# Fewer ordinary gate/up pairs in the SwiGLU stages of a four-layer streaming encoder, and the token-half sums moved within them

## The reference, cut to what matters

```python
def swiglu_ffn(x, w_in, w_out):
    g, u = jnp.split(x @ w_in, 2, axis=-1)
    return (jax.nn.silu(g) * u) @ w_out

    xp = xp + swiglu_ffn(rmsnorm(xp, ffn_norms[i]), *ffn_params[i])
...
y_prompt = rmsnorm(xp, final_norm)
```

## Time and profile before

| | us |
|---|---|
| median of 3 runs | 2585.49 |
| lowest, highest | 2583.73, 2587.84 |
| the profiled execution, device time | 2584.34 |
| its span in the profile | 2582.6 |
| PE busy | 2549.6 (99%) |
| PEld busy | 2483.3 (96%) |
| DVE busy | 1688.8 (65%) |
| ACT busy | 1179.4 (46%) |

### The profile page before, as it was taken

The page is one execution under the profiler, slowest core; times in us unless marked ns, Lnnn a source line. Parts: engine busy times, 40 slices in busy tenths (PEclk is TensorE's granted clock), DMA queues, the critical chain, the costliest instruction groups (busy, mean ns, idle before and its releaser), DMA issues.

```text
span 2582.6 us, 48134 instructions
## 1 busy us (share of the span) xinstructions
PE 2549.6 (99%) x20065; PEld 2483.3 (96%) x20065; DVE 1688.8 (65%) x2465; ACT 1179.4 (46%) x1778; POOL 171.9 (7%) x182
## 2 busy tenths in 40 slices
PE   8999999999999999999999999999999999999998
PEld 8999999999988899999998899999999999999998
DVE  5555793884555579479557556947955555884872
ACT  5454551543555555245345644524524553541443
POOL 2101000001000010000112210000011101000001
PEclk9999999999999999999999999999999999999999
DMA  4222333332433233333222222333322223333322
GB/s 117 70 76 82 99 93 96 99 95 73 124 99 104 77 92 96 91 102 93 84 69 80 72 86 76 97 98 93 100 81 79 72 73 90 98 92 96 94 84 80
DMA packets 441634, 230.68 MB, mean 89 GB/s; under 512 B 16884, under 2 KB 437968, under 8 KB 441440
## 3 DMA queue, kind: packets, MB, share of 16 engines
q1 hardware_dynamic: 439792, 226.89, 30.7%
q10 hardware_dynamic: 1200, 0.59, 0.1%
q0 software_dynamic: 448, 0.45, 0.1%
HBM read 219.03 MB, written 8.87 MB: 88 GB/s over the span
## 4 chain that ended last, share of the span: by engine, by line
PE 95%; DVE 3%; issue 1%; ACT 1%; DMA 0%; DVEq 0%; ACTq 0%
PE slot L2255 53%; PE aux L2734 14%; PE slot L2734 14%; PE aux L2255 4%; PE aux L2223 2%; PE aux L2636 1%; PE aux L2400 1%; PE aux L2642 1%; PE aux L2548 1%; PE aux L2486 1%; DVE w_lo L1397 1%; PE aux L2415 1%; PE aux L2418 0%; PE slot L2695 0%; PE aux L2290 0%
## 5 line engine op out<-in xcount | busy, mean ns | idle before, releaser
L734 ACT ACTIVATE w_hi<-raw 128x1024 fp32r<-128x1024 f32 (+5 forms) x231 | 265.3, 1148 | 346.9 <-PE slot L2255 315.0
L2255 PE MATMUL slot<-xg_hi,w_hi 128*128 128x272 f32 x1856 | 401.8, 298 | 12.5 <-DVE w_lo L1397 10.0
L2255 PE MATMUL slot<-xg_hi,w_lo 128*128 128x272 f32 x1856 | 383.8, 288 | 0.0
L2255 PE MATMUL slot<-xg_lo,w_hi 128*128 128x272 f32 x1856 | 383.7, 288 | 0.0
L1397 DVE TENSOR_TENSOR w_lo<-raw,w_hi 128x1024 fp32r<-128x1024 f32 (+4 forms) x229 | 309.7, 1352 | 69.3 <-ACT w_hi L734 68.6
L2255 PEld LDWEIGHTS slot<-xg_hi,w_hi 128*128 128x128 f32 x1856 | 291.1, 189 | 25.1 <-DVE w_lo L1397 12.4
L2255 PEld LDWEIGHTS slot<-xg_lo,w_hi 128*128 128x128 f32 x1856 | 291.9, 189 | 0.0
L2255 PEld LDWEIGHTS slot<-xg_hi,w_lo 128*128 128x128 f32 x1856 | 290.8, 189 | 0.0
L2255 PE MATMUL slot<-h_hi,w_hi 128*128 128x272 f32 x1386 | 286.1, 288 | 0.7 <-issue 0.7
L2255 PE MATMUL slot<-h_hi,w_lo 128*128 128x272 f32 x1386 | 285.9, 287 | 0.0
L2255 PE MATMUL slot<-h_lo,w_hi 128*128 128x272 f32 x1386 | 285.6, 287 | 0.0
(11 more groups left out here) (391 smaller groups left out, 5859.3 us busy)
## 6 DMA issues: line engine op xcount, KB each, us to landing
raw<-in_l_ffn_w_out_dram SPq DMA_DIRECT2D x64, 704.0 KB, 4.6
raw<-in_l_ffn_w_in_dram SPq DMA_DIRECT2D x72, 512.0 KB, 4.6
raw<-in_l_gla_w_in_dram SPq DMA_DIRECT2D x48, 512.0 KB, 3.8
ffn_raw_b<-in_l_ffn_w_in_dram SPq DMA_DIRECT2D x70, 256.0 KB, 3.5
ffn_raw_b<-in_l_ffn_w_in_dram SPq DMA_DIRECT2D x35, 512.0 KB, 5.2
raw<-in_l_ffn_w_in_dram SPq DMA_DIRECT2D x68, 256.0 KB, 3.3
raw<-in_l_att_w_qkv_dram SPq DMA_DIRECT2D x24, 512.0 KB, 3.8
raw<-in_l_lru_w_in_dram SPq DMA_DIRECT2D x24, 512.0 KB, 3.8
```

Source lines behind the costliest of these rows:

```text
L734: act.activation(w_hi[par][:, 0:kt, :], raw[par][:, 0:kt, :], ACT.Copy).then_inc(s_hi, 1)
L2255: ins = pe.matmul((slot[par] if bank is None else bank)[:, hf, 0:HALF], w[par][:, k, :], a[:, k0 + k, hf * HALF:(hf + 1) * HALF], start=(k ...
```

## The change

Half 0 has now two ordinary pairs and nine seven-product pairs (before 3 and 8), half 1 eleven seven-product pairs (before 1 and 10), and half 1 of the last layer eleven as well (before 4 ordinary and 7 seven-product). Quarters 0 and 1 of t stand in window 0 ahead of the read and the split, quarter 2 in window 0 behind them, quarter 3 in window 1. In half 1 the first pair's weight sums are formed in the last window of down0. The last half's h is no longer multiplied by rstd; its down stage does it, in a read and an add per block.

```diff
-UP_PAIRS = ("CCCSSSSSSSS", "CSSSSSSSSSS")
-LAST_PAIRS = "CSSCSSCSSCS"
-T_PART = {0: (0,), 1: (1, 2), 2: (3,)}
+UP_PAIRS = ("CCSSSSSSSSS", "SSSSSSSSSSS")
+LAST_PAIRS = "SSSSSSSSSSS"
+T_PART = {0: ((0, 1), (2,)), 1: ((3,), ())}
...
         def next_k(i, name):
+            if name == "down0" and up_kinds(i, 1, layers)[0] == "S":
+                return "seven"
...
 # ACT, last_project
-                    act.wait_ge(s_free, b0 + m + 1)
+                    act.wait_ge(s_xd, XT * (2 * i + 1) + m + 1)
...
 # ACT, project_out
-                        split(b0 + m2 * 2 + (j + 1), (p0 + j + 1) % 2, nxt if j else kt)
+                        if j and nxt == "seven":
+                            hi_sums((i, 1, 0), b0 + XT, None)
+                            hi_more_sums((i, 1, 0), b0 + XT, None)
+                        else:
+                            split(b0 + m2 * 2 + (j + 1), (p0 + j + 1) % 2, nxt if j else kt)
...
 # ACT, up_window (DVE's the same with t_low)
-                for q in T_PART.get(u, ()) if hf == 0 else ():
+                for q in T_PART[u][0] if hf == 0 and u in T_PART else ():
                     t_high(i, q)
...
                     split(b + 2, p0, XT if nxt else FH)
                 if now == "C":
                     silu(i, hf, u, kinds)
+                for q in T_PART[u][1] if hf == 0 and u in T_PART else ():
+                    t_high(i, q)
...
 # DVE, last_project, blocks 0 to 6
-                    dve.tensor_tensor(halves(one(x, m)), slot[(b0 + m) % 2][:, :, 0:HALF], halves(one(x, m)),
-                                      ALU.add).then_inc(s_free, 1)
+                    if m:
+                        dve.wait_ge(s_xd, XT * (2 * i + 1) + m)
+                    dve.tensor_tensor(FF["y"][:, 0:2, :], slot[(b0 + m) % 2][:, :, 0:HALF], halves(rstd[:, :]),
+                                      ALU.mult).then_inc(s_free, 1)
+                    dve.wait_ge(s_free, b0 + m + 1)
+                    dve.tensor_tensor(one(x, m), FF["g"], one(x, m), ALU.add).then_inc(s_xd, 1)
...
 # DVE, last_project, each column part of block 7
-                    dve.tensor_tensor(one(x, m, cols), slot[(b0 + m) % 2][:, c, 0:cols.stop - cols.start], one(x, m, cols),
-                                      ALU.add).then_inc(s_ea, 1)
+                    dve.tensor_tensor(FF["u"][:, cols], slot[(b0 + m) % 2][:, c, 0:cols.stop - cols.start], rstd[:, cols],
+                                      ALU.mult).then_inc(s_free, 1)
+                    dve.wait_ge(s_free, b0 + m + 1 + c)
+                    dve.tensor_tensor(one(x, m, cols), FF["u"][:, cols], one(x, m, cols), ALU.add).then_inc(s_ea, 1)
...
 # DVE, project_out
-                        split(b + 1, (p0 + j + 1) % 2, nxt if j else kt)
+                        if j and nxt == "seven":
+                            w_sums((i, 1, 0), b0 + XT)
+                            lo_sums((i, 1, 0), b0 + XT)
+                            lo_more_sums((i, 1, 0), b0 + XT, 2)
+                        else:
+                            split(b + 1, (p0 + j + 1) % 2, nxt if j else kt)
...
 # DVE, product
-                if (i, hf) == (last, 1):
-                    if kinds[u] == "S":
-                        dve.wait_ge(s_h, h_no[at] - 1)
-                    else:
-                        dve.wait_ge(s_free, b + 2)
-                    dve.tensor_tensor(FF["u"], FF["u"], rstd[:, :], ALU.mult).then_inc(s_h, 1)
...
 # PE
+                            if hf == 0 and u == 2:
+                                pe.wait_ge(s_rstd, stat_of[i, "ffn"] + 1)
                             seven_products(i, hf, u, b)
```

More of the change, by code:

```diff
@@ L168, in up_plan @@
         for hf in range(2):
-            run, scaled = 0, (i, hf) == (layers - 1, 1)
+            run = 0
             for u, kind in enumerate(up_kinds(i, hf, layers)):
-                h_count[i, hf, u] = max(h_count.values(), default=0) + (kind == "S") + scaled
+                h_count[i, hf, u] = max(h_count.values(), default=0) + (kind == "S")
                 run = run + 1 if kind == "S" else 0
@@ L1281, in h_high @@
             def h_high(i, hf, u, kinds):
-                if kinds[u] == "S" or (i, hf) == (last, 1):
+                if kinds[u] == "S":
                     act.wait_ge(s_h, h_no[i, hf, u])
@@ L1310, in up_window @@
                 if now == "S":
-                    if prev == "C":
+                    if prev != "S":
                         hi_a11(at, b, prev)
@@ L2084, in c_d_added @@
                 dve.wait_ge(s_hlo, (2 * at[0] + at[1]) * FH + at[2])
+                if at[2] == 0:
+                    dve.wait_ge(s_xd, XT * (2 * at[0] + 1))
                 cd = up_banks(at[1], at[2], p0)[0]
@@ L2175, in up_window @@
                         lo_sums(after, b + 2)
-                    h_low(i, hf, u - 1)
+                    if u:
+                        h_low(i, hf, u - 1)
                     if nxt == "S":
@@ L2199, in up_window @@
                     split(b + 2, p0, XT if nxt else FH)
+                for q in T_PART[u][1] if hf == 0 and u in T_PART else ():
+                    t_low(i, q)
             for i in range(layers):
@@ L2743, in from_x @@
                     return (lambda k: xg_hi[:, k0 + k, cols]), (lambda k: xg_lo[:, k0 + k, cols])
-                a11_second = up_kinds(i, hf, layers)[u - 1] == "S"
+                a11_second = u > 0 and up_kinds(i, hf, layers)[u - 1] == "S"
                 pe.wait_ge(s_free, b - 2)
```

## The result

The changed kernel took 2602.80 us (median of 4 runs, 2600.91 to 2604.48) against 2584.94 us for the kernel before on the same chip: ratio 1.0067, 95% interval 1.0050 to 1.0085. It is slower, by some 17.9 us between medians; 2601 was forecast.

The account below looks back on a forecast made before the run. PE's matmuls plus short stalls at up0's first pair changes were taken as the bound. +25.2 (up0) - 4.5 (up1) - 6.0 (last half) + 0.9 (end) = +15.6 us, forecasting 2601 us, range 2593 to 2610.

Parts of the forecast that it names:

- Matmuls removed: On PE, 11 pairs turned seven-product, 12 matmuls or 1.5 us each: 16.6 us saved if nothing else moves.
- Up0's chain: In each half 0, serial quarters on ACT and DVE delay PE's pairs 1 and 2: 6.3 us a layer, 25.2 in all.
- The 1.0 us at pair 1's second block: In up0, PE waits 1.0 us for DVE's split, queued behind quarter 2, where no wait came before.
- this cover: In up0, pair 1 has 1.0 + 3.4 us to spare before pair 2 moves, covering some 4.4 us of half-clock loss.
- The clock: In pair 2 of up0, two of four layers again meet the half clock, 1.5 us each; total loss 25.2 us.
- Half 1's first pair: Weight sums, about 5.6 us, fit DVE's idle 5.63 us in down0's last window; failed cover costs about 1 us a layer.
- The first pair waits: Rival: sums at down0's end come 1 us late in four layers, giving 2605 us; chance 0.08.
- The end: In down1's last block, the additional DVE operations cost 0.9 us, between 0.45 and 1.0.
- Quarters back to back: Rival: ACT's part of a quarter passes under DVE's previous one in up0; -22.3 us, 2563 us; chance 0.03.
- Only matmuls: Rival: up0's stalls stay as they are and 16.6 - 0.9 us go, giving 2570 us; chance 0.05.
- Half clock more often: Rival: all four layers meet it in pair 2, +3.0 us, 2604; near 2610 if pair 1's cover fails; chance 0.18.

Follow-up runs that it names:

- half 1 alone: Kernel before with only the eleven seven-product pairs in half 1 and the last down stage's two-step reads; half 0 and quarters unchanged: 2577.09 us, ratio 0.9962.
- the repeat: The changed kernel run once more without any edit, against the kernel before: 2601.95 us, ratio 1.0071.
- Quarter 0 early: Half 1 as changed, three ordinary pairs in half 0, DVE's part of quarter 0 put ahead of the rstd copy: 2571.90 us, ratio 0.9955 to the kernel before.

## Why the prediction was right

The forecast was 2601, the time is 2602.8. The steps, in its order:

- *Matmuls removed.* 132, as counted, and a seven-product pair still takes 10.55 us. What the turned pairs are worth by themselves showed in half 1 alone: 9.6 us expected, 8.7 to 9.8 found.
- *Up0's chain.* Forecast and measured offsets in layer 1: quarter 1 at 5.62 and 5.60, the split 10.33 and 10.29, PE's pair 1 11.60 and 11.56, quarter 2 12.69 and 12.64, quarter 3 19.49 and 19.43, the sums 23.57 and 23.49, pair 2 28.06 and 28.07. Adding neighbouring starts of one trace along the new order of the lists was enough, because each list is strictly in order. Up0 as a whole, from quarter 0 to down0's first matmul, took 116.67, 116.66, 118.19 and 118.18 us in the four layers before and 123.09, 124.49, 124.50 and 123.09 after: 25.5 us more, 25.2 forecast. Layer 1's rows, before and after:

```profile
1045.91 0.29 PE L2255 MATMUL slot<-h_hi,w_hi 128*128 128x272 f32 x1
...
1062.76 0.29 PE L2273 MATMUL slot<-h_hi,w_hi 128*128 128x272 f32 x1
```

- *Waits that came smaller.* The 1.0 us at pair 1's second block is absent, and ahead of pair 2 it is 1.8 to 2.9 us and not 3.4. The half clock stretched pair 1 and took that place. The forecast had named this cover and not drawn the conclusion for the waits.
- *A reading that was too even.* The forecast gave all four layers of the kernel before 1.91 us ahead of pair 2. Layer 0 had 0.52, which is why the four sum to 6.3 and not to 7.6. Pair 1 met a half clock there (first row: 14 matmuls in 2.5 us, a mean clock of 0.59), and pair 2 started at 20.19 all the same. So the kernel before already showed that a half clock in pair 1 is covered:

```profile
277.00:279.50 2.50, 2.50 (x14) 2.50 (x14) 2.46 (x4) 1.42 (x3) 0.00 (x0) 0.59 0.84 230
...
290.08 0.36 PE L2255 MATMUL aux<-xg_hi,w_hi 128*128 128x272 f32 x1 [0.52 <-issue]
```

- *The clock.* Two of four layers with a half clock in pair 2 were assumed, and the profile has two (layer 1's pair 2 took 978.49 - 966.34 = 12.15 us against 10.55); the repeat had one. That the number fitted is luck, worth 1.4 us a layer; nothing in the forecast told how many it would be. All four long waits ended in a half clock. That agrees with the rule of the Trainium skill ("TensorE: Matmul & The Clock Gate", "Why this matters for your kernels") against gaps of some microseconds between matmul bursts. Of the eight waits ahead of pair 2 in the two profiles of the changed kernel, those of 2.67, 2.72 and 2.92 us did, and those of 1.49 to 2.13 did not. The first three stood in layers where pair 1 had met 6.8 us of half clock, the others where it had met 10.2, which had used up more of the wait. What a half clock cost depended on its place: in pair 1 it was free, in pair 2, without cover, it was 1.3 to 2.8 us a layer.
- *Half 1's first pair.* The sums fill DVE's window: they end at 461.49 and DVE is idle for 1.83 us before the last block's read, where 5.63 stood. Up1's first matmul (463.13) follows its predecessor (462.87, two matmuls) without a gap. "The first pair waits" falls.

```profile
460.27 1.22 DVE L2077 TENSOR_TENSOR w_lo<-ffn_w_sums,w_hi 128x1024 fp32r<-128x1024 f32 x1
463.32 0.72 DVE L2015 TENSOR_TENSOR ffn_y<-slot,rstd 128x544 f32<-128x544 f32 x1 [1.83 <-PE slot L2273]
```

- *The end.* DVE's timeline of the last block's last part, against the earlier trace rows: a read and an add in the place of one add. From PE's last block to the issue of the last output DMA it is 14.73 us against 13.78: +0.95, 0.9 forecast.

```profile
2594.01 0.36 DVE L1994 TENSOR_SCALAR end_rows<-aux,inv 32x128 f32<-32x128 f32 x1
2594.40 0.42 DVE L1977 TENSOR_TENSOR ffn_y<-slot,rstd 128x256 f32<-128x256 f32 x1
2594.86 0.42 DVE L1980 TENSOR_TENSOR x<-ffn_y,x 128x256 f32<-128x256 f32 x1
```

- *The rivals.* "Quarters back to back" would have put pair 2 at 19.3; it is at 28.07. "Only matmuls" counts the gain right and misses the chain. "Half clock more often" did not occur in the changed kernel, but did in two of the experiments.

What is left between 2601 and 2602.8 is in the range of one kernel's runs: the eight profiled executions whose code is the same up to layer 0's quarter 0 reached it anywhere from 269.9 to 275.2 us. The two without a half clock in their first 50 us did so at 269.9 and 271.0, the one with one such stretch at 271.2, and the five with two at 273.5 to 275.2; whether the clock is the cause was not tested.

## What to carry to other kernels

Before an engine that is busy for 99% of the span is given less work, look at what its long pieces cover: here an ordinary pair cost 1.5 us more than its replacement and was the 12 us under which a serial chain of two other engines ran. When such a chain is the bound, moving its links about moves the wait and not the end; shorten it (a second buffer, an early link in a window where its engine waits anyway) and only then look for the place. Quarter 0 early gave 2 to 5 us on the run with half 1 alone; with two buffers added it was 12 to 15 us, since the first had left a wait of 2.4 us that the second cut to 0.9, along with the half clock behind it. The buffers alone were run only with two ordinary pairs (3 us in the medians), so what they give alone in the kernel with three is not shown.

## What the runs showed of the hardware

The cost of TensorE's half clock depended on its place. Behind waits of 7.7 us it was there in all four layers and cost nothing, because the next waits shrank by as much. In pair 2, right ahead of work without slack, it cost 1.3 to 2.8 us a layer (6.7 us and 9.5 us in two kernels), more than the 6.0 us that four turned pairs save. Filling the waits with throwaway matmuls held the clock at 1.0 through all of half 0. It took away the 1.4 us of each layer in which pair 2 had met the half clock, and changed the median by 0.2 us, less than can be told from the spread of the runs.
